# Weight-panel sums formed by GpSimd in its copy order in a two-block residual layer

## The chip, the cores and the metric

One core of a Trainium2 chip runs the whole kernel. The metric is the device time of one execution in microseconds (us); the time of a kernel is the median of several executions. Five engines work side by side, each through its own queue in order: TensorE (PE, with its weight loads as PEld), VectorE (DVE), ScalarE (ACT), GpSimd (POOL) and SyncE (SP). SP and POOL issue the transfers that matter here.

## The reference

The input is `x`, 2048 positions by 1024 channels, in float32. The part in which the change lies is the gated MLP:

```python
v = rms_norm(h, g_ffn[i])
up = causal_dwconv(v @ w_up[i], w_conv_ffn[i], b_conv_ffn[i])
gate = up[..., :D_FF]
val = up[..., D_FF:]
h = h + (jax.nn.gelu(gate) * val) @ w_down[i]
```

`D_FF` is 3072, and the convolution has 3 taps. Before it come a norm, an input projection, a recurrence, a pooling branch and an output projection; behind it a gated embedding and a last norm.

## The kernel before: panels, sums and queues

The sequence is worked in two blocks of 1024 positions. Weights come as panels of 128x512 (`raw`, 256 KB each, a ring of 5 buffers, loaded by SP in a fixed order). Every panel is split into a high part, written by ACT (`hi(n)`, L888), and a low part, written by DVE (`lo(n)`, L1385: panel minus high part), in a ring of 4 pairs `wpair`; TensorE multiplies in three passes over the two. In block 0 POOL copies each finished pair to DRAM (L588), and block 1 reads them back, so that splitting is done once. `hi(n)` waits until TensorE is through with panel n-4 and until the copy of panel n-4 has landed.

The up projection has 24 output tiles q, in chunks of four. From q = 2 on, gate and value of a tile are computed together by seven products P1, P5, P6, P3, P7, P2, P4 in place of eight. Three panels of the seven are plain ones (P1, P2, P4); the other four are sums or differences of raw panels, formed one after another in the one buffer `wsum`: P5 from two raw panels, P6 from `wsum` and the first raw panel, P3 from the fourth raw panel and `wsum`, P7 from the first and second raw panels. `wsummed(n)` (L1364) forms one, on DVE:

```python
if SUMS[n] > 1:
    dve.wait_ge(panel_lo, max(i for i in range(n) if PANEL_SUM[i] is not None) + 1)
```

that is, it waits until the low part of the sum ahead has been taken, since that reads the same `wsum`. DVE's order is written out by hand. In `pair(b, q)` (L1849) the sums for P3 and P7 of tile q stand around the convolutions of tile q-1 (`gate_conv` L1648 and L1650, `val_conv` L1655 and L1657) and its product `f_tile` (L1663); the sums of the next tile's P5 and P6 stand between `c12_out` (L1773), `c22_out` (L1778) and `c11_out` (L1783), which add a finished product from PSUM. ACT's order in `pair` (L1234) has, between its `hi` calls, `gelu`, the copies out of PSUM `snap_p1` (L1125), `snap_p5` (L1133) and `snap_u2` (L1138), and after `hi` of the next P6 the call `gate_sum` (L1086), which starts the convolution. TensorE may begin P6 after `snap_p1`, P3 after `snap_p5` and P7 after `snap_u2`.

After each chunk comes the down projection, with 8 tiles m and 8 plain panels in two groups of four ("11", "12", "21", "22"). In five of its six chunks four sums of each group (S1 to S4, `down_sums` L1671) are formed for block 1: S1 in `wsum`, the others in the raw buffers themselves. POOL sends them to DRAM after the copy of panel "21" (L594, L597). SP loads the next raw panel into a buffer only when its last reader is through (`panels_to`, L519): low parts taken, and for a buffer with a sum, the sum sent.

## Time and profile before

| | |
|---|---|
| Median of 3 runs | 2172.31 us (2171.94 to 2173.50) |
| The profiled execution, its own time | 2173.85 us |
| Its span in the profile | 2172.1 us |
| TensorE busy | 2129.6 us (98%) |
| VectorE busy | 1434.4 us (66%) |
| ScalarE busy | 859.2 us (40%) |
| GpSimd busy | 353.7 us (16%) |

The span is what the engines' records cover; the own time of the execution is a little longer. A busy share is an average over stages, and TensorE's idle time lies in few places. A row of the timeline reads: start in us, duration in us, engine, line, operation, output<-inputs with their shapes, and in brackets how long the engine sat idle before it and what ended that. In the groups the numbers are the busy time in us, the mean of one in ns, and the idle time just before them.

### The profile page before, as it was taken

What the parts mean: (1) busy time and instruction counts of PE and PEld (TensorE: products, weight loads), DVE (VectorE), ACT (ScalarE), POOL (GpSimd) and SP (SyncE); (2) the same over time, 40 slices, a digit from 0 to 9 for tenths busy, and PEclk for the clock granted to TensorE, in tenths of its full rate; (3) what the DMA queues carried; (4) which work ended last, traced back from release to release, by engine and by line L of the source; (5) the groups of instructions that cost most, each with busy time, mean ns of one, the idle gap of its engine ahead of it and who ended that gap; (6) DMA issues with size and microseconds to landing.
All of it is one profiled execution on the core that took longest, in us unless ns stands there. A gap on an engine that the chain in (4) does not pass through costs nothing.

```text
span 2172.1 us, 24231 instructions
## 1 busy us (share of the span) xinstructions
PE 2129.6 (98%) x9320; PEld 1751.5 (81%) x9320; DVE 1434.4 (66%) x1622; ACT 859.2 (40%) x1119; POOL 353.7 (16%) x662
## 2 busy tenths in 40 slices
PE   7999999999999999999999999999999999999996
PEld 5877887888888888888888888888888888888884
DVE  6875388585867768686777743775655656575646
ACT  4674365252525344354445632531313131313322
POOL 0101101111121212110100010122222222221100
PEclk9999999999999999999999999999999999999998
DMA  5436445664666656576534354466666666666353
GB/s 220 160 117 252 176 178 208 227 250 179 250 231 228 237 223 230 203 283 224 186 122 144 97 203 127 144 194 194 193 192 194 195 192 192 194 194 193 111 176 107
DMA packets 132850, 413.84 MB, mean 191 GB/s; under 512 B 15104, under 2 KB 15232, under 8 KB 132736
## 3 DMA queue, kind: packets, MB, share of 16 engines
q0 software_dynamic: 89632, 313.57, 41.7%
q1 hardware_dynamic: 40800, 90.33, 12.8%
q10 hardware_dynamic: 2304, 8.39, 1.0%
q8 instruction: 75, 1.23, 0.2%
q14 instruction: 39, 0.32, 0.0%
HBM read 241.31 MB, written 170.92 MB: 190 GB/s over the span
## 4 chain that ended last, share of the span: by engine, by line
PE 89%; issue 7%; DVE 2%; DMA 1%; POOL 1%; ACT 0%; SPq 0%; DVEq 0%; POOLq 0%; ACTq 0%
PE slot L628 41%; PE slot L732 38%; PE slot L812 9%; POOL wpair L613 1%; DMA XN<-xT 1%; PE slot L659 1%; DVE H L1999 0%; PE slot L674 0%; DVE wpair L1385 0%; DMA raw<-panels 0%; DVE H L1585 0%; DMA wpair<-split_panels 0%; DVE Ulo L1414 0%; DVE H L1581 0%; SPq L529 0%
## 5 line engine op out<-in xcount | busy, mean ns | idle before, releaser
L732 PE MATMUL slot<-ops,wpair 128*128 128x512 f32 x3696 | 843.4, 390 | 2.8 <-DVE WV L1778 2.4
L732 PEld LDWEIGHTS slot<-ops,wpair 128*128 128x128 f32 x3696 | 694.4, 188 | 149.8 <-DVE WV L1778 2.9
L628 PE MATMUL slot<-Uhi,wpair 128*128 128x512 f32 x1248 | 342.5, 393 | 18.5 <-DVE wpair L1385 12.1
L628 PE MATMUL slot<-f_split,wpair 128*128 128x512 f32 x1344 | 305.8, 389 | 0.0
L628 PEld LDWEIGHTS slot<-f_split,wpair 128*128 128x128 f32 x1344 | 252.3, 188 | 52.3
L628 PEld LDWEIGHTS slot<-Uhi,wpair 128*128 128x128 f32 x1248 | 234.9, 189 | 72.0 <-issue 17.8
L588 POOL DMA_DIRECT2D split_panels<-wpair x274 | 146.1, 534 | 868.8 <-DVE wpair L1385 862.5
L613 POOL DMA_DIRECT2D wpair<-split_panels x264 | 142.2, 539 | 785.2 <-PE slot L628 389.5
L888 ACT ACTIVATE wpair<-raw 128x512 fp32r<-128x512 f32 x186 | 113.6, 624 | 261.6 <-PE slot L628 180.8
L628 PE MATMUL slot<-Ulo,wpair 128*128 128x512 f32 x624 | 193.3, 391 | 0.0
L812 PE MATMUL slot<-f_quarter,wpair 128*128 128x512 f32 x840 | 191.2, 389 | 0.0
L812 PEld LDWEIGHTS slot<-f_quarter,wpair 128*128 128x128 f32 x840 | 157.7, 188 | 32.7
L628 PE MATMUL slot<-Yhi,wpair 128*128 128x512 f32 x608 | 165.2, 389 | 1.9 <-DVE Ylo L1595 1.7
L1385 DVE TENSOR_TENSOR wpair<-raw,wpair 128x512 fp32r<-128x512 f32 x186 | 124.7, 686 | 22.8 <-ACT wpair L888 22.4
L628 PEld LDWEIGHTS slot<-Ulo,wpair 128*128 128x128 f32 x624 | 117.7, 189 | 24.7
L628 PEld LDWEIGHTS slot<-Yhi,wpair 128*128 128x128 f32 x608 | 114.0, 188 | 26.2 <-DVE Ylo L1595 2.1
L1908 DVE TENSOR_TENSOR H<-slot,H 128x1024 f32<-128x1024 f32 x56 | 68.4, 1222 | 97.8 <-PE slot L628 97.2
L1086 ACT ACTIVATE AG<-WG,par 128x1024 f32<-128x1024 f32 x48 | 59.7, 1244 | 156.5 <-DVE WG L1783 149.9
L888 ACT ACTIVATE wpair<-wsum 128x512 fp32r<-128x512 f32 x88 | 55.4, 629 | 146.0 <-DVE wsum L1379 86.5
L1773 DVE TENSOR_TENSOR WG<-slot,WG 128x512 f32<-128x512 f32 x44 | 30.4, 692 | 115.9 <-PE slot L732 115.9
L1731 DVE TENSOR_TENSOR H<-slot,H 128x512 f32<-128x512 f32 x140 | 88.4, 679 | 13.4 <-PE slot L812 13.4
L628 PE MATMUL slot<-Ylo,wpair 128*128 128x512 f32 x304 | 93.6, 389 | 0.0
(187 smaller groups left out, 2252.9 us busy)
## 6 DMA issues: line engine op xcount, KB each, us to landing
split_panels<-wpair POOLq DMA_DIRECT2D x274, 512.0 KB, 4.7
wpair<-split_panels POOLq DMA_DIRECT2D x264, 512.0 KB, 3.6
raw<-panels SPq DMA_DIRECT2D x208, 256.0 KB, 4.3
wpair<-down_sums POOLq DMA_DIRECT2D x40, 256.0 KB, 2.9
wlo_sum<-down_sums POOLq DMA_DIRECT2D x40, 256.0 KB, 3.0
H<-xT SPq DMA_DIRECT2D x8, 1024.0 KB, 12.1
pp_kept<-XQ ACTq DMA_DIRECT2D x16, 512.0 KB, 4.1
PPR<-pp_kept SPq DMA_DIRECT2D x16, 512.0 KB, 4.4
```

The lines of the kernel that those rows point to most:

```text
L588: pool.dma_start(split_d[n], wpair[n % RING][:].bitcast(F32)).then_inc(split_kept[n % RING], 16)
L613: pool.dma_start(wpair[n % RING][:], split_d[KEPT_AT[n]]).then_inc(split_in[n % RING], 16)
L628: mm = pe.matmul(ps[:, h * BANK:(h + 1) * BANK], stat_[:, w], mov(part, h), start=first and i == 0, stop=last and i == 2)
L659: mm = pe.matmul(psum(key)[:, half_of(h)], stat_[:, w], (lo if part else hi)[:, i * KP + k, half_of(h)], start=i == 0 and k == 0 and j == ...
L732: mm = pe.matmul(ps, stat_[:, w], (lo if part else hi)[:, k, :], start=first and k == 0 and i == 0, stop=k == KP - 1 and i == 2, skip_grou ...
L812: mm = pe.matmul(ps, stat_[:, w], f_quarter[:, DOWN_AT[name], part, k, :], start=first and k == 0 and at_pass == 0, stop=k == 1 and at_pas ...
L888: nc.scalar.activation(whi[n % RING], source(n), ACT.Copy).then_inc(panel_hi, 1)
L1086: nc.scalar.activation(AG[:, 0:BLOCK], WG[:, HALO_FFN:HALO_FFN + BLOCK], ACT.Identity, bias=tap(q, 0, 3), scale=tap(q, 0, 2)).then_inc(g_s ...
L1385: v.tensor_tensor(wlo[n % RING], source(n), f32(whi[n % RING]), ALU.subtract).then_inc(panel_lo, 1)
L1731: v.tensor_tensor(dst, psum(key)[:, half_of(column)], dst, ALU.add).then_inc(signal, 1)
L1773: v.tensor_tensor(dst, psum(key)[:, 0:BANK], dst, ALU.add).then_inc(slot_free[SLOT[key]], 1)
L1908: v.tensor_tensor(H[:, m, :], psum(key)[:], H[:, m, :], ALU.add).then_inc(slot_free[SLOT[key]], 1)
```

## The change

All sums of block 0 move from DVE's queue to POOL's. `wsummed(n + 1)` now stands in POOL's loop ahead of the wait for the low part of panel n and the copy of panel n. The down sums (`down_sum`) are formed by POOL too, each just ahead of the transfer that sends it. The formulas and the waits on semaphores are the same otherwise; SP has one more wait, since a raw panel "22" is now read by S1 on POOL. DVE keeps the low parts and all else, in the same order.

```diff
--- before.py
+++ after.py
@@ -264,6 +264,7 @@
 SUM_PLACE = {"S2": "11", "S3": "21", "S4": "12"}
 SUM_RAW = {RAW_AT["down", c, i, kind]: (c, i, name) for c in range(BY_SEVEN) for i in range(2)
            for name, kind in SUM_PLACE.items()}
+SUM_READ = {RAW_AT["down", c, i, "22"]: (c, i) for c in range(BY_SEVEN) for i in range(2)}
...
@@ -526,6 +527,9 @@
                         sync.wait_ge(sum_kept[r % RAW_RING], 16 * SUM_OUT[r - RAW_RING])
                     elif r >= RAW_RING:
                         sync.wait_ge(panel_lo, RAW_FREE[r - RAW_RING])
+                        if r - RAW_RING in SUM_READ:
+                            c, i = SUM_READ[r - RAW_RING]
+                            sync.wait_ge(sums_formed, 4 * (2 * c + i) + 1)
...
@@ -581,14 +585,57 @@
 
         @block.gpsimd
         def _(pool):
+            def wsummed(n):
+
+                if PANEL_SUM[n] is None:
+                    return
+                left, right = PANEL_SUM[n]
+                for r in (left, right):
+                    if r is not None:
+                        pool.wait_ge(*landed(r))
+                if n > PANEL[0, "down", 0, 0, "11"]:
+                    pool.wait_ge(first_sum_kept, 16 * 2 * sum(PANEL[0, "down", c, 0, "11"] < n for c in range(BY_SEVEN)))
+                if SUMS[n] > 1:
+                    pool.wait_ge(panel_lo, max(i for i in range(n) if PANEL_SUM[i] is not None) + 1)
+                first = wsum[:] if left is None else raw[left % RAW_RING][:]
+                second = wsum[:] if right is None else raw[right % RAW_RING][:]
+                plus = left is not None and right == left + 1 and RAW_WHAT[left][0] == "val"
+                nc.gpsimd.tensor_tensor(wsum[:], first, second, ALU.add if plus else ALU.subtract).then_inc(panel_sum, 1)
...
+            def down_sum(c, i, name):
+
+
+                at_raw = {kind: raw[RAW_AT["down", c, i, kind] % RAW_RING][:] for kind in DOWN_KINDS}
+                before = 4 * (2 * c + i)
+                if name == "S1":
+                    pool.wait_ge(*landed(RAW_AT["down", c, i, "22"]))
+                    if c or i:
+                        pool.wait_ge(first_sum_kept, 16 * (2 * c + i))
+                    nc.gpsimd.tensor_tensor(wsum[:], at_raw["21"], at_raw["22"], ALU.add).then_inc(sums_formed, 1)
+                elif name == "S3":
+                    pool.wait_ge(sums_formed, before + 1)
+                    nc.gpsimd.tensor_tensor(at_raw["21"], at_raw["11"], at_raw["21"], ALU.subtract
...
 
             sums_behind = {PANEL[0, "down", c, i, "21"]: (c, i) for c in range(BY_SEVEN) for i in range(2)}
             for n in range(SPLIT):
+                if n + 1 < SPLIT:
+                    wsummed(n + 1)
                 pool.wait_ge(panel_lo, n + 1)
                 pool.dma_start(split_d[n], wpair[n % RING][:].bitcast(F32)).then_inc(split_kept[n % RING], 16)
...
                     c, i = sums_behind[n]
                     for k, name in enumerate(("S1", "S3", "S2", "S4")):
+                        down_sum(c, i, name)
                         pool.wait_ge(sums_formed, 4 * (2 * c + i) + k + 1)
                         if name == "S1":
                             pool.dma_start(sums_d[c, i, 0], wsum[:]).then_inc(first_sum_kept, 16)
...
-            def wsummed(n):
...
-                v.tensor_tensor(wsum[:], first, second, ALU.add if plus else ALU.subtract).then_inc(panel_sum, 1)
...
             def refill(*key):
                 for n in FREED.get(key, ()):
-                    wsummed(n)
                     lo(n)
...
-                wsummed(n0 + 3)
                 if follows:
                     gate_conv(b, q - 1)
                     val_conv(b, q - 1)
                 lo(n0 + 3)
-                wsummed(n0 + 4)
                 if follows:
                     f_tile(b, q - 1)
                 lo(n0 + 4)
...
-                wsummed(n0 + 7)
                 lo(n0 + 7)
-                wsummed(n0 + 8)
                 c22_out(b, q)
                 lo(n0 + 8)
-                wsummed(n0 + 9)
                 c11_out(b, q)
                 lo(n0 + 9)
...
-                    sums = b == 0 and c < BY_SEVEN
-                    if sums:
-                        down_sums(c, 0, ("S1", "S3"))
...
-                        if b == 0 and c < BY_SEVEN and m == 3:
-                            first, second = FREED[key]
-                            lo(first)
-                            down_sums(c, 1, ("S1", "S3", "S2", "S4"))
-                            lo(second)
-                        elif m < DT - 1 or c == CHUNKS - 1:
+                        if m < DT - 1 or c == CHUNKS - 1:
                             refill(*key)
                         else:
                             for n in FREED.get(key, ())[:1]:
-                                wsummed(n)
```

VectorE, from the P6 sum for tile 10 on, in `pair`. The numbers behind names are buffers. Before:

```order
L1385 TENSOR_TENSOR wpair1_78<-wsum_72,wpair1_78 128x512
L1379 TENSOR_TENSOR wsum_72<-wsum_72,raw4_71 128x512
L1783 TENSOR_TENSOR WG_81<-slot0,WG_81 128x512
L1385 TENSOR_TENSOR wpair2_79<-wsum_72,wpair2_79 128x512
L1379 TENSOR_TENSOR wsum_72<-raw2_69,wsum_72 128x512
L1648 SCALAR_TENSOR_TENSOR AG_83<-WG_81,par_85,AG_83 128x1024
L1650 SCALAR_TENSOR_TENSOR AG_83<-WG_81,par_85,AG_83 128x1024
L1655 SCALAR_TENSOR_TENSOR AV_84<-WV_82,par_85,AV_84 128x1024
L1657 SCALAR_TENSOR_TENSOR AV_84<-WV_82,par_85,AV_84 128x1024
L1385 TENSOR_TENSOR wpair3_80<-wsum_72,wpair3_80 128x512
L1379 TENSOR_TENSOR wsum_72<-raw4_71,raw0_67 128x512
L1663 TENSOR_TENSOR AV_84<-AG_83,AV_84 128x1024
```

With the change:

```order
L1415 TENSOR_TENSOR wpair1_78<-wsum_72,wpair1_78 128x512
L1789 TENSOR_TENSOR WG_81<-slot0,WG_81 128x512
L1415 TENSOR_TENSOR wpair2_79<-wsum_72,wpair2_79 128x512
L1677 SCALAR_TENSOR_TENSOR AG_83<-WG_81,par_85,AG_83 128x1024
L1679 SCALAR_TENSOR_TENSOR AG_83<-WG_81,par_85,AG_83 128x1024
L1684 SCALAR_TENSOR_TENSOR AV_84<-WV_82,par_85,AV_84 128x1024
L1686 SCALAR_TENSOR_TENSOR AV_84<-WV_82,par_85,AV_84 128x1024
L1415 TENSOR_TENSOR wpair3_80<-wsum_72,wpair3_80 128x512
L1692 TENSOR_TENSOR AV_84<-AG_83,AV_84 128x1024
```

The three sums (L1379) are gone from DVE's queue, and each low part of a sum (L1385, now L1415, from `wsum`) now has only a wait for ACT's high part ahead of it.

GpSimd at the same place, the copies from tile 10's P1 on. Before:

```order
L588 DMA split_panels<-wpair0_77 128x1024
L588 DMA split_panels<-wpair1_78 128x1024
L588 DMA split_panels<-wpair2_79 128x1024
L588 DMA split_panels<-wpair3_80 128x1024
L588 DMA split_panels<-wpair0_77 128x1024
```

With the change:

```order
L603 TENSOR_TENSOR wsum_72<-raw0_67,raw1_68 128x512
L634 DMA split_panels<-wpair0_77 128x1024
L603 TENSOR_TENSOR wsum_72<-wsum_72,raw4_71 128x512
L634 DMA split_panels<-wpair1_78 128x1024
L603 TENSOR_TENSOR wsum_72<-raw2_69,wsum_72 128x512
L634 DMA split_panels<-wpair2_79 128x1024
L603 TENSOR_TENSOR wsum_72<-raw4_71,raw0_67 128x512
L634 DMA split_panels<-wpair3_80 128x1024
L634 DMA split_panels<-wpair0_77 128x1024
L634 DMA split_panels<-wpair1_78 128x1024
```

The four sums of tile 10 (L603) stand ahead of the copies of P1, P5, P6 and P3 (L634).

GpSimd in the down projection of the chunk, first group. Before:

```order
L588 DMA split_panels<-wpair0_77 128x1024
L594 DMA down_sums<-wsum_72 128x512
L597 DMA down_sums<-raw4_71 128x512
L597 DMA down_sums<-raw2_69 128x512
L597 DMA down_sums<-raw3_70 128x512
L588 DMA split_panels<-wpair1_78 128x1024
```

With the change:

```order
L634 DMA split_panels<-wpair0_77 128x1024
L614 TENSOR_TENSOR wsum_72<-raw4_71,raw0_67 128x512
L641 DMA down_sums<-wsum_72 128x512
L617 TENSOR_TENSOR raw4_71<-raw2_69,raw4_71 128x512
L644 DMA down_sums<-raw4_71 128x512
L621 TENSOR_TENSOR raw2_69<-wsum_72,raw2_69 128x512
L644 DMA down_sums<-raw2_69 128x512
L625 TENSOR_TENSOR raw3_70<-raw3_70,raw2_69 128x512
L644 DMA down_sums<-raw3_70 128x512
L634 DMA split_panels<-wpair1_78 128x1024
```

A sum (L614 to L625) stands ahead of each of the four transfers, and the copy of panel "22" is the first behind all four.

## Rows read from the trace of the kernel before

**Rows 1.** The page: busy time by engine (busy us, share of the span, instructions).
```profile
PE 2129.6 (98%) x9320; PEld 1751.5 (81%) x9320; DVE 1434.4 (66%) x1622; ACT 859.2 (40%) x1119; POOL 353.7 (16%) x662
```

**Rows 2.** Busy us by stretch: length, PE, PEld, DVE, ACT, POOL; clock, DMA share, GB/s.
```profile
346.00:1024.00 678.00, 677.96 (x2977) 559.73 (x2978) 488.30 (x580) 282.61 (x433) 127.24 (x238) 1.00 0.62 231
```

**Rows 3.** Groups by line and shape: count, busy us, mean ns, idle before and releaser.
```profile
L732 PE MATMUL slot<-ops,wpair 128*128 128x512 f32 x3696 | 843.4, 390 | 2.8 <-DVE WV L1778 2.4 <-ACT WG L1138 0.3
...
L588 POOL DMA_DIRECT2D split_panels<-wpair x274 | 146.1, 534 | 868.8 <-DVE wpair L1385 862.5 <-issue 4.3
...
L1663 DVE TENSOR_TENSOR AV<-AG,AV 128x1024 f32<-128x1024 f32 x33 | 40.3, 1220 | 0.3
...
L1379 DVE TENSOR_TENSOR wsum<-raw,raw 128x512 f32<-128x512 f32 x44 | 30.3, 689 | 7.3 <-DMA raw<-panels 3.1 <-issue 1.2
...
L1638 DVE TENSOR_TENSOR UN<-UN 128x2048 f32<-128x2048 f32 x8 | 18.3, 2284 | 0.0
```

**Rows 4.** Timeline, 559 us to 580 us, pairs 9 and 10: start, us, engine, line, operation.
```profile
559.62 0.69 DVE L1385 TENSOR_TENSOR wpair<-wsum,wpair 128x512 fp32r<-128x512 f32 x1
...
564.72 0.69 DVE L1379 TENSOR_TENSOR wsum<-raw,raw 128x512 f32<-128x512 f32 x1
...
567.62 0.69 DVE L1379 TENSOR_TENSOR wsum<-wsum,raw 128x512 f32<-128x512 f32 x1
...
568.85 0.63 ACT L888 ACTIVATE wpair<-wsum 128x512 fp32r<-128x512 f32 x1 [2.09 <-PE slot L732]
...
569.51 0.69 DVE L1385 TENSOR_TENSOR wpair<-wsum,wpair 128x512 fp32r<-128x512 f32 x1
...
569.73 1.24 ACT L1086 ACTIVATE AG<-WG,par 128x1024 f32<-128x1024 f32 x1
570.34 0.69 DVE L1379 TENSOR_TENSOR wsum<-raw,wsum 128x512 f32<-128x512 f32 x1
570.50 0.53 POOL L588 DMA_DIRECT2D split_panels<-wpair  x1 [2.18 <-DVE wpair L1385]
571.00 1.29 DVE L1648 SCALAR_TENSOR_TENSOR AG<-WG,par,AG 128x1024 f32<-128x1024 f32 x1
...
576.10 0.68 DVE L1385 TENSOR_TENSOR wpair<-wsum,wpair 128x512 fp32r<-128x512 f32 x1
576.91 0.69 DVE L1379 TENSOR_TENSOR wsum<-raw,raw 128x512 f32<-128x512 f32 x1
...
577.52 1.22 DVE L1663 TENSOR_TENSOR AV<-AG,AV 128x1024 f32<-128x1024 f32 x1
...
578.66 0.68 DVE L1385 TENSOR_TENSOR wpair<-wsum,wpair 128x512 fp32r<-128x512 f32 x1
...
579.74 0.59 ACT L1138 ACTIVATE WG<-slot 128x512 f32<-128x512 f32 x1
```

**Rows 5.** DMA issues, 560.0 us to 561.5 us: count, KB, us to landing.
```profile
raw<-panels SPq DMA_DIRECT2D x2, 256.0 KB, 3.4
```

**Rows 6.** Timeline, 633 us to 659 us: down projection, then first pair q = 12.
```profile
633.27 0.69 DVE L1682 TENSOR_TENSOR wsum<-raw,raw 128x512 f32<-128x512 f32 x1
...
644.03 0.68 DVE L1379 TENSOR_TENSOR wsum<-raw,raw 128x512 f32<-128x512 f32 x1
...
656.60 0.69 DVE L1379 TENSOR_TENSOR wsum<-raw,wsum 128x512 f32<-128x512 f32 x1
...
657.95 0.58 ACT L1125 ACTIVATE WG<-slot 128x512 f32<-128x512 f32 x1
...
658.58 1.45 PEld L732 LDWEIGHTS slot<-ops,wpair 128*128 128x128 f32 x7 [0.43 <-ACT WG L1125]
...
658.90 0.69 DVE L1379 TENSOR_TENSOR wsum<-raw,raw 128x512 f32<-128x512 f32 x1
```

**Rows 7.** Timeline, 341 us to 346 us: the end of the first pair by products, q = 2.
```profile
344.65 0.68 DVE L1379 TENSOR_TENSOR wsum<-raw,raw 128x512 f32<-128x512 f32 x1
...
345.99 6.20 PE L732 MATMUL slot<-ops,wpair 128*128 128x512 f32 x19 [2.44 <-DVE WV L1778]
```

More of the change, by code:

```diff
@@ new lines, in down_sum @@
+            def down_sum(c, i, name):
[9 more added lines that the diff above has]
+                    nc.gpsimd.tensor_tensor(at_raw["21"], at_raw["11"], at_raw["21"], ALU.subtract
+                                            ).then_inc(sums_formed, 1)
+                elif name == "S2":
+                    pool.wait_ge(sums_formed, before + 2)
+                    nc.gpsimd.tensor_tensor(at_raw["11"], wsum[:], at_raw["11"], ALU.subtract
+                                            ).then_inc(sums_formed, 1)
+                else:
+                    pool.wait_ge(sums_formed, before + 3)
+                    nc.gpsimd.tensor_tensor(at_raw["12"], at_raw["12"], at_raw["11"], ALU.subtract
+                                            ).then_inc(sums_formed, 1)
@@ L1362, in f32 @@
                 return ap.bitcast(F32)
-            def wsummed(n):
-                if PANEL_SUM[n] is None:
-                    return
-                left, right = PANEL_SUM[n]
-                for r in (left, right):
-                    if r is not None:
-                        dve.wait_ge(*landed(r))
-                if n > PANEL[0, "down", 0, 0, "11"]:
-                    dve.wait_ge(first_sum_kept, 16 * 2 * sum(PANEL[0, "down", c, 0, "11"] < n for c in range(BY_SEVEN)))
-                if SUMS[n] > 1:
-                    dve.wait_ge(panel_lo, max(i for i in range(n) if PANEL_SUM[i] is not None) + 1)
-                first = wsum[:] if left is None else raw[left % RAW_RING][:]
-                second = wsum[:] if right is None else raw[right % RAW_RING][:]
-                plus = left is not None and right == left + 1 and RAW_WHAT[left][0] == "val"
-                v.tensor_tensor(wsum[:], first, second, ALU.add if plus else ALU.subtract).then_inc(panel_sum, 1)
             def lo(n):
@@ L1669, in f_lo_tile @@
                 v.tensor_tensor(dst, src, f32(hi_part), ALU.subtract).then_inc(f_ready, 1)
-            def down_sums(c, i, names):
-                at_raw = {kind: raw[RAW_AT["down", c, i, kind] % RAW_RING][:] for kind in DOWN_KINDS}
-                before = 4 * (2 * c + i)
-                for name in names:
-                    if name == "S1":
-                        dve.wait_ge(panel_lo, PANEL[0, "down", c, i, "21"] + 1)
-                        dve.wait_ge(*landed(RAW_AT["down", c, i, "22"]))
-                        if c or i:
-                            dve.wait_ge(first_sum_kept, 16 * (2 * c + i))
-                        v.tensor_tensor(wsum[:], at_raw["21"], at_raw["22"], ALU.add).then_inc(sums_formed, 1)
-                    elif name == "S3":
-                        v.tensor_tensor(at_raw["21"], at_raw["11"], at_raw["21"], ALU.subtract
-                                        ).then_inc(sums_formed, 1)
-                    elif name == "S2":
-                        dve.wait_ge(sums_formed, before + 2)
-                        v.tensor_tensor(at_raw["11"], wsum[:], at_raw["11"], ALU.subtract).then_inc(sums_formed, 1)
-                    else:
-                        dve.wait_ge(sums_formed, before + 3)
-                        v.tensor_tensor(at_raw["12"], at_raw["12"], at_raw["11"], ALU.subtract
-                                        ).then_inc(sums_formed, 1)
             def sum_lo_part(b, c, name, i):
@@ L1815, in second_pair @@
                 t_lo_half(b, T3)
-                wsummed(n0 + 1)
                 gate_conv(b, 1)
@@ L1819, in second_pair @@
                 lo(n0 + 1)
-                wsummed(n0 + 2)
                 f_lo_tile(b, 0)
@@ L1851, in pair @@
                 follows = q % CHUNK != 0
-                wsummed(n0 + 3)
                 if follows:
@@ L1856, in pair @@
                 lo(n0 + 3)
-                wsummed(n0 + 4)
                 if follows:
@@ L1867, in pair @@
                     d_formed(b, q // CHUNK, "T1")
-                wsummed(n0 + 7)
                 lo(n0 + 7)
-                wsummed(n0 + 8)
                 c22_out(b, q)
                 lo(n0 + 8)
-                wsummed(n0 + 9)
                 c11_out(b, q)
@@ L1899, in ffn @@
                     f_tile(b, q)
-                    if sums:
-                        down_sums(c, 0, ("S2",))
                     f_lo_tile(b, q)
-                    if sums:
-                        down_sums(c, 0, ("S4",))
                     for m in range(DT):
```

## The prediction

> **What bounds the kernel now.** I read the page first: TensorE is busy for 2129.6 of 2172.1 us, VectorE for 1434.4 and GpSimd for 353.7 [rows 1]. The table by stretch then shows where TensorE's 42.5 idle us are not: from 346 to 1024 us, the stretch in which all but a few sums are formed, it is busy 677.96 of 678 us at full granted clock, with VectorE at 488.3 us (72%) and GpSimd at 127.2 us [rows 2]. So there is nothing to gain there; a relief of VectorE can pay only ahead of 346 us. The groups say how much: TensorE's matmuls on `ops` sat idle 2.8 us in all, 2.4 of it behind VectorE's L1778 [rows 3], and the timeline shows the spot: at 345.99 TensorE starts after 2.44 us of waiting, and a sum of 0.68 us at 344.65 stands in VectorE's queue just ahead of the awaited add [rows 7]. From 1024 us on no sum is formed.
>
> Since TensorE is full, what counts is how much lateness each consumer can bear. The timeline of tiles 9 and 10 [rows 4] is the pattern. The low part of the P7 panel comes at 559.62 and again at 578.66: 19.04 us a tile, 2.72 us a product. Everything hangs on one loop per tile. When the low part of P7 is done (560.31), SP may load the raw panels for the next P5; they land 3.4 us after issue [rows 5]. Then come the P5 sum (564.72), its high and low part, the P6 sum (567.62), high part (568.85) and low part (569.51), `gate_sum` (569.73), the P3 sum (570.34), four convolution instructions from 571.00, the low part of P3 (576.10), the P7 sum (576.91, ended 577.60), and after it on ScalarE `snap_u2` (579.74 to 580.33). TensorE ended P2 of tile 9 at 568.85 and so ends P3 of tile 10 five products later, at 582.45, and needs `snap_u2` then. The P7 sum may thus be 582.45 - 580.33 = 2.1 us later than now. In the loop ScalarE twice idles 2.09 us for TensorE (one of these is the row at 568.85); that, less what the sums take meanwhile, is the loop's spare, about 1 us.
>
> **The change, part by part.**
>
> *Removed from VectorE:* 128 sums (88 here, the first of three shapes with 44 of 689 ns [rows 3], and 40 down sums) at 0.69 us, 88 us. In the full stretch they save nothing, because TensorE sets the pace.
>
> *Added to GpSimd:* the same 128. No row shows GpSimd computing. From below, VectorE's 0.69 us for this shape; from above, VectorE's 2.28 us for four times the columns [rows 3]. I take 1.22 us, the row of twice the columns, which lies in the middle by ratio. The Trainium skill's GPSIMD Engine Reference (3.1, Elementwise side by side) has a two-input add of 2048 columns at 4497 ns; by a quarter of that, 1.12 us, my sum would come out about 7 us lower, an estimate; no run here shows it yet.
>
> *Hand-over:* GpSimd's copy starts 0.30 us after the low part it waits for (570.20 to 570.50) [rows 4]. I put 0.3 us ahead of each sum that waits for a low part; VectorE had some 0.13.
>
> *Overlap:* a sum on GpSimd now runs beside VectorE. Two of four per tile meet VectorE's work: the P3 sum meets the convolutions, the P7 sum meets `f_tile` (1.22 us), which is no longer behind it. The price lies between nothing and both waiting for each other in full, 1.22 us at each place. No row shows a price below or inside these ends: GpSimd's instructions so far are transfers of 534 ns [rows 3]. I take the upper end. The reason is that the loop turns slower than TensorE for nearly all of the interval: with 16 such tiles, 0.27 us per tile are already 4.3 us, the 0.2% that a measurement of this kernel can tell from no change, and the upper end is 2.4 us per tile.
>
> *The loop added up,* from the end of the P7 low part: raw panels landed 4.1 (two issues, then 3.4); P5 sum 4.3 to 5.5; high and low part, 1.5, to 7.0; P6 sum 7.3 to 8.5; high and low part to 10.0, `gate_sum` (1.24) to 10.4; P3 sum 10.3 to 11.5; convolutions and low part of P3, 5.8 us as now (571.00 to 576.78), from 10.4 to 16.2 if nothing is held up, from 11.5 to 17.3 if turns are taken. Then the P7 sum ends at 17.7 or, behind `f_tile`, at 19.6; now it is 17.3. High and low part close the loop at 19.2 or 21.1, against TensorE's 19.04.
>
> *First tile of a chunk:* it has no convolutions. `snap_p1` ends at 658.53 and TensorE loads for P6 at 658.58, so nothing is spare there [rows 6]; the P6 sum no longer stands behind an add into `H`, which gives back about what the longer P3 sum takes. The P7 sum, now 658.90 to 659.59, ends some 0.8 us later, and the loop starts with that.
>
> *Sum with turns taken:* second tile of a chunk: late by 0.8 + 2.3 against 2.1 allowed, 1.0 us of stall. Third and fourth: 21.1 - 19.04 = 2.0 each. 5.0 us a chunk, five full chunks 25 us, and tile 3 another 1.0. The down projection of 43.5 us (16 products) in between lets the panels catch up.
>
> *Down sums:* one group costs GpSimd about 4 x (1.22 + 0.3 + 0.53 + 0.3) = 9.4 us instead of 3 us behind S1 at 633.27 [rows 6]. S4's transfer and the raw load behind it put the P5 sum of tile 12 near 650 us instead of 644.03. TensorE needs the panel one product before 658.58, at 655.86, and high and low part take 1.5: some 3 us are left. VectorE's last low part ahead of the down projection has about as much, so I add 0.5 us in all. SP's extra wait costs nothing, since S1 is formed first, and it waits for S2 and S4 in any case.
>
> *Before 346 us:* VectorE loses three sums of 0.69, but with turns it waits for as long as it saves. Zero; at best 2.75 us of idle time go.
>
> Together 26.5 us; against the profiled execution 2173.85 + 26.5 = 2200.4, against the median, 1.5 us lower, **2199 us**.
>
> **The rivals.**
> 1. *GpSimd and VectorE do not hold each other up.* Loop 19.2: 0.2 us a tile beyond TensorE's pace, 1.2 to 1.6 us late against 2.1 allowed; no stall. For it: the spare is there, and nothing in the trace shows the two engines meeting. Result 2170 to 2176, no change. The Trainium skill's SBUF page ("SBUF — State Buffer", Who interferes with whom) says that a VectorE instruction with two SBUF inputs and a GpSimd instruction that reads SBUF exclude each other for a whole instruction. By that rule this rival is out and the 2199 stands; no run here shows it yet.
> 2. *The sum is long.* At 2.28 us, without turns, the loop takes 3.2 us more: 22.4, 3.4 a tile, 4.4 for the second, 11.1 a chunk, plus 1.1 at each chunk's start where nothing is spare: 60 + 5, about 2237. With turns too, beyond 2270. Against it: an engine of the chip taking more than three times VectorE's 0.69 us for one pass over 512 columns would be slow.
> 3. *Not slower: VectorE's relief pays.* Below 346 us VectorE is back to back, and the sum at 344.65 directly delays what TensorE awaits [rows 7]. With a sum of under 1 us and no turns, three sums leave its queue and up to 2.75 us of idle time vanish: 2169.6. It decides only if the loop stays under 19.04 us, that is if a sum takes less than about 1.15 us unhindered. It would still be within 0.2%.
> That the sums don't move can be excluded: both queues' orders show it.
>
> **How the numbers follow.** Turns taken 0.52, no holding up 0.30, a long sum 0.12, relief 0.06. Slower by over 0.2%: 0.52 + 0.12, and 0.02 from a lighter holding up in rival 1, 0.66. Within: 0.32. Faster: 0.02, since nothing but the 2.75 us is there to be had. With turns, a sum of 1.0 us gives a loop of 20.2 and 10 us in all, one of 1.5 us a loop of 22.2 and 47 us: the forecast's own range is 2182 to 2220. The 8-in-10 range goes from rival 1's low end to the long sum: 2170 to 2240.
>
> **What the profile will show.** Right: L603 on GpSimd near 1.2 us alone and about twice that beside `f_tile`, or convolutions (L1677 to L1686) well above 1.28 us; TensorE idle in the second to fourth tile of each chunk behind ScalarE's `snap_u2`, 5 us a chunk; none in the down projections. Wrong: VectorE's two-input rows at 0.69, 1.22 and 1.28 us unchanged beside GpSimd's sums; a sum over 1.5 us; TensorE waiting at chunk starts or for a low part instead; idle time below 346 us gone.

## The result, and the profile after

The changed kernel takes 2214.84 us (median of 4 runs, 2214.32 to 2217.94), the kernel before on the same chip 2172.9 us (4 runs): 1.019 times as long, interval 1.0178 to 1.0202, some 42 us. Forecast were 2199.0 us and 26.5 us more. The direction and the range were right, the size was too small.

The page of the changed kernel, busy us by engine, answers to [rows 1]:

```profile
PE 2143.0 (97%) x9320; PEld 1753.3 (79%) x9320; DVE 1386.4 (63%) x1494; ACT 855.7 (39%) x1119; POOL 539.4 (24%) x790
```

And the same stretch as [rows 2], length, PE, PEld, DVE, ACT, POOL, clock, DMA share, GB/s:

```profile
346.00:1024.00 678.00, 648.64 (x2806) 526.06 (x2805) 409.45 (x430) 256.94 (x407) 299.98 (x355) 0.99 0.58 218
```

TensorE, which had no idle time here, is now idle for 678 - 648.64 = 29.4 us; VectorE is busy 79 us less in this stretch, and nobody gains from it. In the whole page it is busy 48 us less, where its 128 sums had taken 88: the other 40 us are rows of its own that became longer. GpSimd gained 186 us in the page, nearly all of it for the 128 sums, 1.44 us each on average. The groups of the changed kernel (answering to [rows 3]) say why the mean is so high, and whose lateness TensorE waits for:

```profile
L779 PE MATMUL slot<-ops,wpair 128*128 128x512 f32 x3696 | 851.5, 391 | 24.9 <-ACT WG L1172 12.9 <-ACT WG L1185 10.9 <-DVE WV L1784 1.0
...
L675 PE MATMUL slot<-f_split,wpair 128*128 128x512 f32 x1344 | 309.0, 391 | 6.3 <-DVE f_split L1698 6.3
...
L1677 DVE SCALAR_TENSOR_TENSOR AG<-WG,par,AG 128x1024 f32<-128x1024 f32 x48 | 75.9, 1581 | 45.7 <-ACT AG L1133 45.6
L603 POOL TENSOR_TENSOR wsum<-raw,raw 128x512 f32<-128x512 f32 x44 | 72.3, 1642 | 142.7 <-DVE wpair L1415 91.0 <-DMA raw<-panels 51.6
...
L1679 DVE SCALAR_TENSOR_TENSOR AG<-WG,par,AG 128x1024 f32<-128x1024 f32 x48 | 66.2, 1380 | 1.7
...
L603 POOL TENSOR_TENSOR wsum<-raw,wsum 128x512 f32<-128x512 f32 x22 | 29.1, 1323 | 27.9 <-DVE wpair L1415 27.9
L603 POOL TENSOR_TENSOR wsum<-wsum,raw 128x512 f32<-128x512 f32 x22 | 28.9, 1314 | 23.1 <-DVE wpair L1415 23.1
```

The sums for P6 and P3 (the last two rows) take 1.31 to 1.32 us. The first shape holds P5 and P7, and its mean is 1.64 us: in the timeline 17 of the 22 P7 sums take 2.08 to 2.11 us, the others 1.28. The convolutions, all near 1.28 us before, have means from 1.38 to 1.58 us, although half of the 48 of each line belong to block 1, where no sum is formed. TensorE waits for three results: `snap_p1` (L1172), `snap_u2` (L1185), and the last step ahead of the down projection, `f_split` (L1698).

The timeline of the changed kernel shows one tile, q = 11 (start, us, engine, line, operation, idle before in brackets):

```profile
583.80 0.68 DVE L1789 TENSOR_TENSOR WG<-slot,WG 128x512 f32<-128x512 f32 x1
584.07 1.29 POOL L603 TENSOR_TENSOR wsum<-wsum,raw 128x512 f32<-128x512 f32 x1 [1.13 <-DVE wpair L1415]
...
587.01 1.29 POOL L603 TENSOR_TENSOR wsum<-raw,wsum 128x512 f32<-128x512 f32 x1 [1.12 <-DVE wpair L1415]
587.36 2.02 DVE L1677 SCALAR_TENSOR_TENSOR AG<-WG,par,AG 128x1024 f32<-128x1024 f32 x1 [0.54 <-ACT AG L1133]
589.41 1.28 DVE L1679 SCALAR_TENSOR_TENSOR AG<-WG,par,AG 128x1024 f32<-128x1024 f32 x1
590.73 1.06 ACT L1153 ACTIVATE AG<-AG 128x1024 f32<-128x1024 f32 x1 [1.03 <-DVE AG L1679]
591.69 0.58 ACT L1172 ACTIVATE WG<-slot 128x512 f32<-128x512 f32 x1
592.33 26.39 PE L779 MATMUL slot<-ops,wpair 128*128 128x512 f32 x108 [2.27 <-ACT WG L1172]
593.73 1.22 DVE L1692 TENSOR_TENSOR AV<-AG,AV 128x1024 f32<-128x1024 f32 x1
594.00 2.08 POOL L603 TENSOR_TENSOR wsum<-raw,raw 128x512 f32<-128x512 f32 x1 [5.18 <-DVE wpair L1415]
```

Two instructions are held up, each time the one that starts second. The convolution at 587.36 takes 2.02 us in place of 1.28: the P3 sum ends at 588.30, and the convolution ends 1.08 us after that. The P7 sum at 594.00 takes 2.08 us in place of 1.29: `f_tile` ends at 594.95, the sum 1.13 us after that. The waiting shows as a longer instruction, not as idle time. It is the same in 16 tiles, where the first convolution takes 1.97 to 2.02 us. An add that reads PSUM (583.80, `slot`) and a sum that starts beside it take 0.68 and 1.29 us, what they take alone.

What follows is a queue: the late L1679 makes `gelu` late (590.73), `snap_p1` stands behind `gelu` on ScalarE (591.69), and TensorE waits 2.27 us for it.

The stages, each from the start of its first product in the timeline (us):

| Stage | before | after, chunk by chunk | more |
|---|---|---|---|
| up to the first of the five down projections with sums | 369.5 | 372.5 | 3.0 |
| down projection (five) | 43.5 each | 45.7, 44.6, 44.5, 44.9, 47.3 | 9.5 |
| four tiles of the next chunk (five) | 76.5 each | 83.1, 81.8, 81.3, 83.5, 80.9 | 28.1 |

Together 40.6 us, all of the 2212.7 - 2172.1 us between the two spans.

The timeline of the changed kernel at the third of these down projections shows where its share comes from:

```profile
627.32 2.63 DVE L1677 SCALAR_TENSOR_TENSOR AG<-WG,par,AG 128x1024 f32<-128x1024 f32 x1 [0.80 <-ACT AG L1133]
627.57 1.29 POOL L614 TENSOR_TENSOR wsum<-raw,raw 128x512 f32<-128x512 f32 x1
...
629.76 1.34 POOL L617 TENSOR_TENSOR raw<-raw,raw 128x512 f32<-128x512 f32 x1
629.99 2.20 DVE L1679 SCALAR_TENSOR_TENSOR AG<-WG,par,AG 128x1024 f32<-128x1024 f32 x1
...
631.98 1.36 POOL L621 TENSOR_TENSOR raw<-wsum,raw 128x512 f32<-128x512 f32 x1
632.11 2.32 DVE L1684 SCALAR_TENSOR_TENSOR AV<-WV,par,AV 128x1024 f32<-128x1024 f32 x1
...
634.24 1.34 POOL L625 TENSOR_TENSOR raw<-raw,raw 128x512 f32<-128x512 f32 x1
634.46 2.20 DVE L1686 SCALAR_TENSOR_TENSOR AV<-WV,par,AV 128x1024 f32<-128x1024 f32 x1
...
639.53 1.23 DVE L1698 TENSOR_TENSOR f_split<-AV,f_split 128x1024 fp32r<-128x1024 f32 x1 [1.13 <-ACT f_split L1158]
640.81 4.38 PE L675 MATMUL slot<-f_split,wpair 128*128 128x512 f32 x18 [0.72 <-DVE f_split L1698]
```

All four convolutions of the chunk's last tile meet one of the four down sums each, and lose each time, the first of them although its row starts 0.25 us ahead of the sum's. They take 9.35 us in place of 5.13, and TensorE waits for what comes after them. In three of the five chunks it is the first down sum that loses against the first convolution (at 501.74 it takes 1.94 us, the convolution at 501.24 its 1.28), and the other three convolutions still lose.

Before the full stretch it is the same, with larger instructions (timeline of the changed kernel; the first P7 sum stands behind the product at 335.20 as above):

```profile
335.46 2.10 POOL L603 TENSOR_TENSOR wsum<-raw,raw 128x512 f32<-128x512 f32 x1 [1.34 <-DVE wpair L1415]
...
340.31 7.39 PE L779 MATMUL slot<-ops,wpair 128*128 128x512 f32 x24 [1.84 <-ACT WG L1185]
...
344.10 2.28 DVE L1672 TENSOR_TENSOR ops<-UN,ops 128x2048 fp32r<-128x2048 f32 x1
344.46 3.06 POOL L603 TENSOR_TENSOR wsum<-raw,raw 128x512 f32<-128x512 f32 x1
346.29 1.78 DVE L1415 TENSOR_TENSOR wpair<-raw,wpair 128x512 fp32r<-128x512 f32 x1
```

The P3 sum at 331.40 takes 2.19 us, the convolution at 332.48 2.20 and the P7 sum 2.10, and TensorE waits 1.84 us for `snap_u2`, where it waits 0.31 us (337.82) in the kernel before. At 344.46 the sum waits for the 2.28 us instruction, and then the low part of 0.69 us waits for the sum. This second chain costs TensorE no longer wait than before: the next one is 1.03 us (348.73), against the 2.44 us of [rows 7].

Not all of the 3.0 us up to 372.5 us come from sums. TensorE is 0.9 us behind the kernel before already when it starts the products at 327.40 (326.47 before), and it had not waited since 182 us, while the first sum starts at 315.72. The 0.9 us come with a fall of TensorE's clock, before which it was 0.7 us ahead: from 160 to 172 us its granted clock is 0.86 here and 1.00 in the trace before, and 0.86 also in the trace of `e8_c22_first` below, which has no sum on GpSimd. So the sums account for some 2.1 us here.

### The profile page after: what moved, and what is told of

Read it like the earlier page. It is cut to its first block, busy times and chain, and to the rows that moved or that the text cites. A ratio compares the mean times of both kernels' runs of the same rounds, so it can differ in the third digit from the quotient of the medians.

```text
span 2212.7 us, 24242 instructions
## 1 busy us (share of the span) xinstructions
PE 2143.0 (97%) x9320; PEld 1753.3 (79%) x9320; DVE 1386.4 (63%) x1494; ACT 855.7 (39%) x1119; POOL 539.4 (24%) x790
## 4 chain that ended last, share of the span: by engine, by line
PE 68%; DVE 10%; issue 9%; DMA 5%; POOL 4%; ACT 3%; SPq 0%; POOLq 0%; ACTq 0%; DVEq 0%
PE slot L675 37%; PE slot L779 22%; PE slot L859 9%; POOL wsum L603 3%; DVE wpair L1415 2%; DMA raw<-panels 2%; DVE AG L1677 2%; DMA split_panels<-wpair 2%; DVE AV L1684 1%; DVE AG L1679 1%; ACT AG L1133 1%; ACT wpair L935 1%; POOL wpair L660 1%; DMA XN<-xT 1%; PE slot L706 0%
## 5 line engine op out<-in xcount | busy, mean ns | idle before, releaser
L779 PE MATMUL slot<-ops,wpair 128*128 128x512 f32 x3696 | 851.5, 391 | 24.9 <-ACT WG L1172 12.9
L634 POOL DMA_DIRECT2D split_panels<-wpair x274 | 150.0, 548 | 561.5 <-DVE wpair L1415 554.3
L1415 DVE TENSOR_TENSOR wpair<-raw,wpair 128x512 fp32r<-128x512 f32 x186 | 128.5, 709 | 30.5 <-ACT wpair L935 30.1
L1415 DVE TENSOR_TENSOR wpair<-wsum,wpair 128x512 fp32r<-128x512 f32 x88 | 60.7, 690 | 135.9 <-ACT wpair L935 135.8
L603 POOL TENSOR_TENSOR wsum<-raw,raw 128x512 f32<-128x512 f32 x44 | 72.3, 1642 | 142.7 <-DVE wpair L1415 91.0
L1677 DVE SCALAR_TENSOR_TENSOR AG<-WG,par,AG 128x1024 f32<-128x1024 f32 x48 | 75.9, 1581 | 45.7 <-ACT AG L1133 45.6
```

The costliest lines, as they stand in the source:

```text
L603: nc.gpsimd.tensor_tensor(wsum[:], first, second, ALU.add if plus else ALU.subtract).then_inc(panel_sum, 1)
L634: pool.dma_start(split_d[n], wpair[n % RING][:].bitcast(F32)).then_inc(split_kept[n % RING], 16)
L779: mm = pe.matmul(ps, stat_[:, w], (lo if part else hi)[:, k, :], start=first and k == 0 and i == 0, stop=k == KP - 1 and i == 2, skip_grou ...
L1415: v.tensor_tensor(wlo[n % RING], source(n), f32(whi[n % RING]), ALU.subtract).then_inc(panel_lo, 1)
L1677: chain.link(v.scalar_tensor_tensor(AG[:, 0:BLOCK], WG[:, 1:1 + BLOCK], tap(q, 0, 1), AG[:, 0:BLOCK], ALU.mult, ALU.add))
```

## The experiments

Ratios are against the kernel before on the same chip. Its median was 2174.1 us for the runs up to `e4_memset_in_place`, and 2174.2 to 2174.5 us for the others. The question: is it the turns that the two engines take, or only that a sum is longer on GpSimd and comes later? And which sums cost what?

### Which sums: tiles and down projections apart

**e1_tile_sums_only** keeps the 88 sums of the tiles on GpSimd and gives the 40 down sums back to VectorE (against the changed kernel, in part):

```diff
-                        down_sum(c, i, name)
...
+                    if sums:
+                        down_sums(c, 0, ("S1", "S3"))
```

> The 88 sums of tiles 2 to 23 on GpSimd, the 40 down sums back on VectorE. Turn-taking theory: the stalls in the tiles stay (28 us) and the start's (about 3 us), the ones in the down projections (9.5 us) go: 2172.9 + 31 = about 2204 us. Rival, the down sums' burst starts the lateness that the tiles then carry: below 2190 us.

Measured: 2206.09 us, ratio 1.0143 (1.0127 to 1.0159), 32 us more. The down projections are back at 43.5 us, the stalls in the tiles remain.

**e2_down_sums_only** does the opposite. Against the changed kernel, GpSimd's loop skips the tile sums and VectorE's queue forms them again at the old places (one of them shown):

```diff
+        def on_pool(n):
+            return False
...
-                if PANEL_SUM[n] is None:
+                if PANEL_SUM[n] is None or not on_pool(n):
...
                 for n in FREED.get(key, ()):
+                    wsummed(n)
                     lo(n)
```

> The reverse: only the 40 down sums on GpSimd, the 88 tile sums on VectorE. Turn-taking theory: each of the four convolutions behind a chunk is held up by one sum (2.2 to 2.6 us instead of 1.28), TensorE waits about 1 us in each of five down projections, 5 to 10 us in all: 2178 to 2183 us. Rival, these stalls come from lateness carried in from the tiles: 2173 us, as before.

Measured: 2187.93 us, ratio 1.0064 (1.0049 to 1.0079), 14 us more, where 5 to 10 were expected: a miss in size. The profiled execution was the slowest of the four, 3.6 us above the median. TensorE's rows in its timeline show two costs a chunk:

```profile
634.73 31.58 PE L681 MATMUL slot<-f_split,wpair 128*128 128x512 f32 x138 [0.72 <-DVE f_split L1722]
671.90 71.06 PE L785 MATMUL slot<-ops,wpair 128*128 128x512 f32 x312 [0.15 <-ACT WG L1178]
...
794.08 71.01 PE L785 MATMUL slot<-ops,wpair 128*128 128x512 f32 x312 [1.13 <-ACT WG L1178]
```

One is the wait for `f_split`, from the held convolutions. The other, from 0.15 to 2.45 us, is `snap_p1` in the next chunk's first tile, where nothing was spare [rows 6]: this down projection starts 12 us later than before; the second group of down sums on GpSimd starts at 647.37, and the sum for the next tile's P5, at 644.03 before, is formed at 663.29, so 7 us later than the stage alone makes it, after 6 us of waiting for its raw panel. The five waits of each kind are 3.6 and 7.3 us; two of the tile stages also ran at a granted clock of 0.98, which costs some 3 us (last section). 32 + 14 = 46 us is near the 42 of the whole change: the two parts are about additive.

### Which sums of a tile

The next three leave the down sums on VectorE and use the edit shown in GpSimd's loop, with another condition each (`!= 'P3'` in e5, `!= 'P7'` in e6); VectorE forms the sums that GpSimd does not:

```diff
+        def on_pool(n):
+            return NAMES.get(n) in ('P5', 'P6')
...
-                if PANEL_SUM[n] is None:
+                if PANEL_SUM[n] is None or not on_pool(n):
```

**e3_p5_p6_only**: the two sums of a tile that stand beside neither the convolutions nor `f_tile`.

> Only the P5 and P6 sums (44) on GpSimd, which meet no VectorE instruction with two SBUF inputs in the steady tiles; P3, P7 and the down sums on VectorE. Turn-taking theory: the loop is about 1.4 us longer than before minus its 1 us of spare, inside the 2.1 us allowed: 2173 to 2177 us. Rival, a sum's length and hand-over alone make the loss: half of the sums, about half of it, 2190 us or more.

Measured: 2173.61 us (10 runs), ratio 0.9997 (0.9988 to 1.0006). No change; convolutions at 1281 to 1285 ns. Around the start of a chunk the P5 sum does meet low parts of plain panels (two SBUF inputs as well), and seven of these take 0.96 to 1.74 us in place of 0.69:

```profile
423.88 1.28 POOL L609 TENSOR_TENSOR wsum<-raw,raw 128x512 f32<-128x512 f32 x1 [0.21 <-DMA raw<-panels]
424.18 1.53 DVE L1413 TENSOR_TENSOR wpair<-raw,wpair 128x512 fp32r<-128x512 f32 x1
```

TensorE's only wait of over 0.1 us from 372 to 1020 us is 0.27 us, so these meetings cost nothing. What counts is where a meeting lies, not that there is one.

**e5_all_but_p3**: P5, P6 and P7 on GpSimd.

> P5, P6 and P7 sums on GpSimd, P3 and the down sums on VectorE: of the two places where turns are taken in a tile, only the one behind f_tile is left. Turn-taking theory: compared with the run with P5 and P6 alone the loop gains about 2 us (turn 1.2, length and hand-over 0.8), at most about 1 us of it beyond what is allowed in the third and fourth tile: 2180 to 2190 us. Rival, the convolutions' delay behind the P3 sum is what releases TensorE late (its waits end on snap_p1), so without it nothing is lost: 2173 to 2177 us.

Measured: 2196.49 us, ratio 1.0098 (1.0084 to 1.0112), 22 us more: a miss, twice the middle of what was expected.

**e6_all_but_p7**: P5, P6 and P3 on GpSimd.

> P5, P6 and P3 sums on GpSimd, P7 and the down sums on VectorE: only the turn between the P3 sum and the first convolution is left, about 1 us. Turn-taking theory: the loop gains 1 us, mostly inside what is allowed: 2174 to 2183 us, less than the 32 us of both places and less than the run without P3. Rival (snap_p1 waits for the delayed convolutions): most of the 32 us, 2190 us or more.

Measured: 2181.34 us, ratio 1.003 (1.0017 to 1.0042), 7 us more. So of the 32 us in the tiles the P3 sum is worth about 7, the P7 sum about 22. That P7 costs three times as much fits its place: it is the last in the loop and passes its lateness to the next tile's P5 undiminished, while part of the P3 sum lies beside `gate_sum`. No run tests this reading.

### Turns or length

**e4_memset_in_place** leaves out the arithmetic of all 128 sums: each is replaced by two memsets of its destination, one behind the other, some 1.12 us, that read no SBUF. Everything else stays in its place and order. TensorE then multiplies zeros in these panels.

```diff
+            def stand_in(dst):
+                nonlocal written
+                written += 1
+                nc.gpsimd.memset(dst, 0.0).then_inc(half_written, 1)
+                pool.wait_ge(half_written, written)
+                return nc.gpsimd.memset(dst, 0.0)
...
-                nc.gpsimd.tensor_tensor(wsum[:], first, second, ALU.add if plus else ALU.subtract).then_inc(panel_sum, 1)
+                stand_in(wsum[:]).then_inc(panel_sum, 1)
```

> All 128 sums on GpSimd replaced by two memsets of the same tile in a row, with a wait between, in the same places of the queue and with the same signals: GpSimd writes and does not read SBUF. It leaves out the sums, whose panels become zeros. Turn-taking theory (the second input of VectorE and GpSimd's reads share something): VectorE's rows go back to 1.28 us and the loss falls to 0 to 5 us, if the pair of memsets takes 1.0 to 1.4 us. Rival, length alone: about 2210 us with the same lengths.

Measured: 2170.35 us (10 runs), ratio 0.9982 (0.9972 to 0.9991). Two thirds of the gain lie ahead of 369 us: the wait of [rows 7] is 1.58 us, and TensorE's clock does not fall behind it (see below). Its timeline:

```profile
587.67 0.53 POOL L594 MEMSET wsum<- 128x512 f32 x1 [1.14 <-DVE wpair L1422]
588.06 1.28 DVE L1684 SCALAR_TENSOR_TENSOR AG<-WG,par,AG 128x1024 f32<-128x1024 f32 x1 [0.54 <-ACT AG L1140]
588.25 0.53 POOL L596 MEMSET wsum<- 128x512 f32 x1
```

The same convolution beside a GpSimd instruction that only writes: 1.28 us. But this left two causes mixed, since the pair is also shorter than a sum (1.29 us). The next run did not part them.

**e7_three_memsets**: a third memset, about 1.7 us per stand-in (the sums are left out here too; the diff is against e4).

```diff
-                written += 1
-                nc.gpsimd.memset(dst, 0.0).then_inc(half_written, 1)
-                pool.wait_ge(half_written, written)
+                for _ in range(2):
+                    written += 1
+                    nc.gpsimd.memset(dst, 0.0).then_inc(half_written, 1)
+                    pool.wait_ge(half_written, written)
```

> The run with memsets in place of the sums, with three instead of two in a row, about 1.7 us, longer than a sum of 1.29 us on GpSimd. It leaves out the sums as that run did. Turn-taking theory: VectorE's rows stay at 1.28 us, but the loop of a tile is now longer by its length alone, some 0.6 us at three places: stalls of 1 to 2 us in the later tiles, 2180 to 2200 us. Rival, only turns cost, length is hidden: 2170 to 2174 us.

Measured: 2213.64 us, ratio 1.0181 (1.0165 to 1.0197), 39 us more: a clear miss. The convolutions stay at 1.28 us and the stalls end on `snap_p1` and `snap_u2` as in the changed kernel. Length alone can thus do as much damage, at 1.7 us a sum, and from e4 and e7 it could not be said how much 1.29 us do. Two runs at matched lengths settled it.

**e9_memset_as_long**: the stand-in of e4 and a third, short write (diff against e4). The sums are left out.

```diff
-                return nc.gpsimd.memset(dst, 0.0)
+                nc.gpsimd.memset(dst, 0.0).then_inc(half_written, 1)
+                written += 1
+                pool.wait_ge(half_written, written)
+                return nc.gpsimd.memset(dst[:, 0:64], 0.0)
```

> The change with each of its 128 sums left out and replaced by writes alone, as in e4_memset_in_place, but with a third, short write (64 columns) so that the stand-in takes about 1.3 us, as long as an unhindered sum (1.29 us); the numbers that the sums would give are thus left out. Turns theory (most of the 42 us is time in which GpSimd's sums and VectorE's two-input instructions wait for each other): writes do not meet, so only length is left. Four stand-ins of a tile are some 0.18 us longer each than in e4, 0.5 to 0.7 us a tile, of which TensorE's spare of about 1 us and the 2.1 us allowed take most: 0 to 10 us over before, convolutions at 1.28 us. Rival (length alone does it, as the 39 us of e7_three_memsets at 1.7 us may suggest): 25 to 42 us over before at the same 1.3 us.

Measured: 2181.01 us (5 runs), ratio 1.0032 (1.0018 to 1.0045), 7 us more. Its timeline:

```profile
593.64 0.53 POOL L594 MEMSET wsum<- 128x512 f32 x1 [0.80 <-DVE wpair L1425]
594.03 1.29 DVE L1687 SCALAR_TENSOR_TENSOR AG<-WG,par,AG 128x1024 f32<-128x1024 f32 x1 [0.54 <-ACT AG L1143]
594.23 0.53 POOL L596 MEMSET wsum<- 128x512 f32 x1
594.81 0.15 POOL L599 MEMSET wsum<- 128x64 f32 x1
```

From 593.64 to 594.96 the stand-in takes 1.32 us, a real sum's length, and the convolution beside it 1.29. That one row stands for all: the groups from 346 to 1024 us, of e9 and then of the changed kernel, have the first convolution at

```profile
L1687 DVE SCALAR_TENSOR_TENSOR AG<-WG,par,AG 128x1024 f32<-128x1024 f32 x22 | 28.3, 1285 | 12.3 <-ACT AG L1143 12.3
...
L1677 DVE SCALAR_TENSOR_TENSOR AG<-WG,par,AG 128x1024 f32<-128x1024 f32 x22 | 42.5, 1934 | 12.2 <-ACT AG L1133 12.2
```

The zeros that the stand-ins leave for TensorE don't explain it either: four tiles in which it does not wait take 76.2 us in e9, and as much in e3 with its real sums.

**e10_short_sums**: real sums over 440 of 512 columns, so that one takes 1.13 us, the length of the pair in e4. The last 72 columns are left out (the buffer `wsum` is filled with zeros once at the start).

```diff
+            def part(ap):
+                return ap[:, 0:440]
...
-                nc.gpsimd.tensor_tensor(wsum[:], first, second, ALU.add if plus else ALU.subtract).then_inc(panel_sum, 1)
+                nc.gpsimd.tensor_tensor(part(wsum[:]), part(first), part(second), ALU.add if plus else ALU.subtract).then_inc(panel_sum, 1)
```

> The change with real sums over 440 of the 512 columns (the last 72 columns of each sum are left out), so that a sum takes about 1.12 us unhindered, as long as the pair of writes of e4_memset_in_place, which cost nothing (ratio 0.998). Turns theory: the sums still hold up convolutions (1.28 to 2 us and more) and are held up by f_tile, so 12 to 30 us over before. Rival (length alone): no change, within 4 us of before.

Measured: 2198.76 us, ratio 1.0116 (1.0102 to 1.0129), 25 us more. Its timeline:

```profile
600.49 1.13 POOL L610 TENSOR_TENSOR wsum<-raw,wsum 128x440 f32<-128x440 f32 x1 [1.49 <-DVE wpair L1422]
600.84 1.85 DVE L1684 SCALAR_TENSOR_TENSOR AG<-WG,par,AG 128x1024 f32<-128x1024 f32 x1 [0.54 <-ACT AG L1140]
...
607.05 1.22 DVE L1699 TENSOR_TENSOR AV<-AG,AV 128x1024 f32<-128x1024 f32 x1
607.32 1.94 POOL L610 TENSOR_TENSOR wsum<-raw,raw 128x440 f32<-128x440 f32 x1 [5.17 <-DVE wpair L1422]
```

Put side by side, as us more than before:

| | about 1.12 us | about 1.3 us | about 1.7 us |
|---|---|---|---|
| writes alone, nothing held up | -4 (e4) | +7 (e9) | +39 (e7) |
| real sums, turns taken | +25 (e10) | +42 (the change) | not run |
| share of the turns | 28 | 35 | |

At a sum's own length some 35 of the 42 us come with the turns, and 7 are length. The rival, that length alone does it (25 to 42 us expected of e9), falls. The first row also shows how near the edge the loop was: 0.2 us more per sum cost 11 us, 0.4 us on top of that another 32, which is about four sums a tile times 0.4 us times 20 tiles.

### What could be had

**e8_c22_first** takes the kernel before and puts, in the first pair by products, the add that TensorE waits for [rows 7] ahead of the low part and the sum:

```diff
+                c22_out(b, q)
                 lo(n0 + 7)
                 wsummed(n0 + 8)
-                c22_out(b, q)
                 lo(n0 + 8)
```

> The kernel before with one edit: in the first tile by products VectorE adds the product that TensorE waits for ahead of the next panel's low part and sum, and not behind them. The 2.4 us wait at 346 us should fall to about 1.1 us: 1 us faster than before, 2173 us against 2174, hardly measurable. If the raw panel's landing is what that wait rests on, nothing changes.

Measured: 2173.23 us (11 runs), ratio 0.9994 (0.9985 to 1.0002). The row that answers to [rows 7], in its timeline:

```profile
345.52 4.85 PE L732 MATMUL slot<-ops,wpair 128*128 128x512 f32 x20 [1.24 <-DVE WV L1778]
```

The wait falls from 2.44 to 1.24 us as meant, but 1.2 us are 0.06% of the whole, less than such a comparison can tell. Part of it also comes back: the sums behind are later now, and with them the convolutions and `snap_p1`, for which TensorE waits 1.36 us at 355.36, where it waited for nothing before.

**e11_p5_p6_c22_first** joins the harmless part of the change (e3) with this.

> The version that might beat both: only the sums for P5 and P6 of each tile on GpSimd (e3_p5_p6_only, no change) and in the third part of the first pair c22_out ahead of the low part and sum in front of it (e8_c22_first, no change but 1.2 us less idle time at 345.5 us). Every theory: 2170 to 2175, ratio 0.998 to 1.001; if both small reliefs add up, 1 to 2 us faster, which is at the edge of what can be measured.

Measured: 2172.41 us (11 runs), ratio 0.9995 (0.9987 to 1.0004). No measurable gain. Its trace shows that the two do not add up. The P5 sum on GpSimd (343.03, 1.30 us) now meets the large VectorE instruction that stands ahead of the awaited add, this takes 3.79 us in place of 2.28, and the wait that e8 had shortened to 1.24 us is 2.73 us:

```profile
342.70 3.79 DVE L1671 TENSOR_TENSOR ops<-UN,ops 128x2048 fp32r<-128x2048 f32 x1
...
347.14 1.85 PE L760 MATMUL slot<-ops,wpair 128*128 128x512 f32 x6 [2.73 <-DVE WV L1806]
```

No version that forms real sums on GpSimd beat the kernel before.

## Why the prediction was right, and where its size was off

*What bounds the kernel.* Right: TensorE full from 346 us on, so less work for VectorE brings next to nothing there: where nothing on the path is held up (e3, e4), four tiles take 76.2 to 76.4 us, before 76.5. e4 shows the most that the relief was worth with unhindered stand-ins of 1.12 us: 4 us. "At full granted clock" was read from a rounded 1.00 [rows 2]: from 345 to 350 us of the kernel before the clock is 0.66. The 96 products behind the 2.44 us wait take 23.65 us; the 192 after them take 43.68, so 96 at full clock take 21.8. That wait cost some 4 us, not 2.4, which is one reason why e4 gained more than the 2.75 us of idle time.

*"The upper end: turns are taken".* Right, and the choice that decided the sign: e9 and e10 show it at matched lengths. The rule of the Trainium skill that stood beside it ("SBUF — State Buffer", Who interferes with whom) holds here in both directions, and in its narrow form: VectorE with two SBUF inputs against GpSimd reading SBUF. The add with one input from PSUM (583.80) and the memsets of e4 were not held up.

*The price of a meeting, 1.22 us at each place.* Too high for the tiles: the second to start waits only for what is left of the first, and then takes somewhat less than its own length: 0.74 us for the convolution at 587.36 and 0.79 for the sum at 594.00, 1.5 a tile against the 2.4 that I took. In the down projection at 627 us it is nearer, 1.05 us each.

*The sum, 1.22 us.* Measured 1.28 to 1.32 alone. The estimate of 1.12 us from the Trainium skill's GPSIMD Engine Reference was lower still. On this loop that matters: by e4 and e9, some 0.2 us more per sum are 11 us.

*The raw panels "landed 4.1", with 3.4 us from issue [rows 5].* Too low in part. The issues of the changed kernel from 573 to 600 us read (count, KB, us to landing)

```profile
raw<-panels SPq DMA_DIRECT2D x6, 256.0 KB, 4.8
```

and those of the kernel before in the same stretch 3.9. Over the whole page it is 4.3 us in both, so 3.4 us, taken from two issues, was low for the kernel before too.

*The loop, 21.1 us.* At q = 11 the low part of P7 comes at 596.86 and next at 617.41: 20.55 us. The loop ahead of it, from 574.18 to 596.86, took 22.7 us, with GpSimd waiting 2.81 us for a raw panel at 581.13. Smaller terms (the meetings) and larger ones (sum, landing) nearly cancel: 26 us were summed for the tiles, 28.1 came, with one fall of the clock among them. That the sum for the tiles came out so near is luck in part.

*"The allowance of 2.1 us at the P7 sum", stalls behind `snap_u2`.* Only half right. `snap_p1` (12.9 us) ended more of TensorE's waits than `snap_u2` (10.9). It stands on ScalarE behind `gelu`, which the held convolutions make late. I had followed the loop through the panels, and not the second path, through the convolutions' results.

*Down sums, 0.5 us.* **The step that failed most: 9.5 us,** 1.6 of them a fall of the clock (last section). I counted how long GpSimd and the transfers take and when the next P5 sum comes, but not whom the sums meet. They start at 627.57 and lie on all four convolutions of the chunk's last tile. e2 shows it alone, with 14 us, and that the next chunk's first tile pays too when its panels come late. "None in the down projections" was wrong.

*Before 346 us, zero.* 3.0 us up to 372.5, of which 0.9 were there ahead of any effect of a sum. The rest is mainly the 1.84 us wait at 340.31 for `snap_u2`, behind the held-up P3 and P7 sums: the pattern of the later tiles, already in the first one. The 2.75 us of idle time did not go but moved.

*The forecast's own terms* thus give 28.1 in place of 26, 9.5 in place of 0.5 and 3.0 in place of 0. Of the missing 14 us, 9 are in the down projections, where I had not asked which instruction runs beside the sum; the rest is spread, and falls of TensorE's clock are part of it.

## What to carry to other kernels

Before an operation moves to another engine, list for every place what the first engine does at that moment and which operands both read; count meetings by place, in all stages, not only in the one that is hardest to keep in time. A loop between engines with less than 1 us to spare per turn has no room for a slower engine, even where that engine is three quarters idle. Where two causes fit (length, contention), run a stand-in of equal length that lacks only the one. A meeting off the path costs nothing (e3), and two small gains can undo each other (e11), so look at the trace of the joined version and not only at its time.

## What was not expected of the hardware

GpSimd's memset of 128x512 takes 0.53 us and held up VectorE in no row of e4, e7 and e9; its sum of the same shape takes 1.29 us and met it in each row shown here by holding it up or being held up, where VectorE's instruction had two SBUF inputs.

TensorE's clock fell in two of the ten stages between 372 and 1010 us, after stretches of waits. In the table by stretch the fifth down projection has a granted clock of 0.96 (length, PE, PEld, DVE, ACT, POOL, clock, DMA share, GB/s):

```profile
881.87:929.19 47.32, 45.50 (x193) 37.05 (x192) 24.27 (x21) 9.06 (x13) 21.33 (x25) 0.96 0.49 179
```

Its rows among TensorE's in the timeline of the changed kernel, beside those of the first down projection:

```profile
386.75 31.59 PE L675 MATMUL slot<-f_split,wpair 128*128 128x512 f32 x138 [1.82 <-DVE f_split L1698]
...
896.16 33.20 PE L675 MATMUL slot<-f_split,wpair 128*128 128x512 f32 x138 [1.82 <-DVE f_split L1698]
```

The same 138 products after the same wait of 1.82 us take 31.59 us at full clock and 33.20 us with the fall. So a stall can cost 1.6 us beyond its own length. With two such stages that is some 3 of the 42 us; the trace before has no fall between 372 and 1010 us, but one behind its wait at 345.99. Why it fell behind one wait and not behind the other, the rows here do not tell, nor does one profiled execution tell how often it falls.
